# Block 0's expert rows start behind three heads' query columns, the rest standing between its rows

## The reference, cut to what matters

```python
def peer_ffn(h, w_q, sub_k1, sub_k2, u_tab, v_tab):
    q = (h @ w_q).reshape(B, S, PEER_HEADS, 2, PEER_HALF)
    s1 = jnp.einsum('bshd,hnd->bshn', q[..., 0, :], sub_k1)
    s2 = jnp.einsum('bshd,hnd->bshn', q[..., 1, :], sub_k2)
    v1, i1 = lax.top_k(s1, PEER_TOPK)
    v2, i2 = lax.top_k(s2, PEER_TOPK)
    ...
    top_s, pos = lax.top_k(cand_s, PEER_TOPK)
    idx = jnp.take_along_axis(cand_i, pos, axis=-1)
    wts = jax.nn.softmax(top_s, axis=-1)
    ...
        act = jax.nn.gelu(jnp.einsum('thkd,td->thk', u_tab[ib], xb), approximate=False)
        return jnp.einsum('thk,thkd->td', act * wb, v_tab[ib])

for i in range(DEPTH):
    mix = token_mixer(h, ...)
    h = layer_norm(DEEPNORM_ALPHA * h + mix, ln1_g[i], ln1_b[i])
    ffn = peer_ffn(h, peer_wq[i], peer_k1[i], peer_k2[i], peer_u[i], peer_v[i])
    ple = jax.nn.sigmoid(h @ ple_gate[i]) * (p[i] @ ple_proj[i])
    h = layer_norm(DEEPNORM_ALPHA * h + ffn + ple, ln2_g[i], ln2_b[i])
```

## Time and profile before

| | us |
|---|---|
| median of 3 runs | 2176.77 |
| lowest, highest | 2174.72, 2176.99 |
| profiled execution, span | 2174.5 |
| busy: PE, DVE, ACT, POOL | 1833.6, 1416.6, 1025.8, 760.4 |
| gathered rows, share of 16 DMA engines over the span | 59.3% |
| weights and the like, same | 15.5% |

### The profile page before, as it was taken

One profiled execution on the slowest core, in us unless ns is written; L12 is line 12 of the kernel. 1 busy time (PEld: TensorE's weight loads), 2 busy tenths in 40 slices (PEclk: granted clock), 3 DMA queues, 4 the chain that ended last, 5 costly groups with the idle time before them and its releaser, 6 DMA issues. The chain is left out here.

```text
span 2174.5 us, 29162 instructions
## 1 busy us (share of the span) xinstructions
PE 1833.6 (84%) x7040; PEld 1080.4 (50%) x7040; DVE 1416.6 (65%) x3386; ACT 1025.8 (47%) x2321; POOL 760.4 (35%) x604
## 2 busy tenths in 40 slices
PE   8999998978778788788799999989787887888776
PEld 7987776932222222223288877769322322322222
DVE  5764465587777777776567535555877776877764
ACT  5743444444454444445347344544545544444443
POOL 0010000135555556665300100001466565565562
PEclk9999999999999999999989999999999999999999
DMA  7411444689999999999744124446799999999996
GB/s 258 143 60 60 153 137 146 221 351 427 428 427 428 427 426 428 428 427 428 330 139 146 46 78 136 140 161 242 289 427 428 428 427 427 427 428 427 428 427 292
DMA packets 105487, 656.28 MB, mean 302 GB/s; under 512 B 11712, under 2 KB 11840, under 8 KB 39232
## 3 DMA queue, kind: packets, MB, share of 16 engines
q0 software_dynamic: 74592, 542.36, 59.3%
q1 hardware_dynamic: 30816, 112.91, 15.5%
HBM read 654.17 MB, written 1.05 MB: 301 GB/s over the span
## 5 line engine op out<-in xcount | busy, mean ns | idle before, releaser
L567 PE MATMUL acc<-arena 128*128 128x512 f32 x1536 | 755.8, 622 | 239.3 <-ACT arena L898 238.4
L487 POOL DMA_INDIRECT arena<-experts_dram,stage x384 | 541.3, 1410 | 337.0 <-PE acc L567 228.1
L1215 DVE CUSTOM_DVE_ANT_0 arena<-arena,h 128x1024 f32<-128x1024 f32 x384 | 471.1, 1227 | 253.2 <-DMA arena<-experts_dram,stage 163.0
L567 PEld LDWEIGHTS acc<-arena 128*128 128x128 f32 x1536 | 270.2, 192 | 713.8 <-issue 712.9
L892 ACT ACTIVATE gel<-dots 128x1 f32<-128x1 f32 x512 | 103.1, 201 | 519.6 <-DVE dots L1215 519.0
L1121 DVE TENSOR_TENSOR raw_r<-raw,w_hi 128x1024 fp32r<-128x1024 f32 x200 | 236.6, 1221 | 148.0 <-ACT w_hi L834 146.8
L567 PE MATMUL acc<-hidden,arena 128*128 128x512 f32 x512 | 251.9, 627 | 27.2 <-ACT arena L898 25.8
L834 ACT ACTIVATE w_hi<-raw 128x1024 fp32r<-128x1024 f32 x200 | 202.8, 1053 | 126.6 <-DMA raw<-weights_dram 96.7
L898 ACT ACTIVATE arena<-cst,gw 128x128 f32<-128x128 f32 x512 | 205.6, 402 | 88.1 <-ACT gw L895 41.9
L487 POOL DMA_INDIRECT hidden<-experts_dram,stage x128 | 161.4, 1261 | 136.4 <-PE acc L567 101.4
L1215 DVE CUSTOM_DVE_ANT_0 hidden<-hidden,h 128x1024 f32<-128x1024 f32 x128 | 156.9, 1228 | 66.5 <-issue 39.5
(11 more groups left out here) (248 smaller groups left out, 2241.7 us busy)
## 6 DMA issues: line engine op xcount, KB each, us to landing
raw<-weights_dram SPq DMA_DIRECT2D x208, 512.0 KB, 3.4
arena<-experts_dram,stage POOLq DMA_INDIRECT x384, 13.7
lnr<-lnrows_dram POOLq DMA_DIRECT2D x4, 1024.0 KB, 5.2
hidden<-experts_dram,stage POOLq DMA_INDIRECT x128, 13.7
cst<-consts_dram SPq DMA_DIRECT2D x1, 1640.0 KB, 15.1
par<-params_dram POOLq DMA_DIRECT2D x2, 616.0 KB, 10.5
h<-x_dram SPq DMA_DIRECT2D x2, 512.0 KB, 5.2
out_dram<-h SPq DMA_DIRECT2D x2, 512.0 KB, 5.3
```

Of the source, the lines that this page charges most:

```text
L487: nc.gpsimd.indirect_dma_start(slots[i % RING][:, :], None, experts[:, :], bass.IndirectOffsetOnAxis(stage[:, i:i + 1], 0)).then_inc(slot_ ...
L567: last = mm(acc[:, c * 512:(c + 1) * 512], diag[:, i % 4, :], slots[i % RING][:, D + c * 512:D + (c + 1) * 512], start=False, stop=ends)
L1215: nc.vector.tensor_tensor_reduce(slots[s][:, 0:D], slots[s][:, 0:D], h[:, b, :], 1.0, 0.0, ALU.mult, ALU.add, dots[:, i:i + 1]).then_inc(d ...
```

## The change

Only two `wq` halves and then one more stand ahead of the rows of block 0: heads 0, 1 and 2 (`("wq", 0, 0)`, `("wq", 0, 1)`, `("wq", 1, 0)`), with their scores and the selections of heads 0 and 1. The rows of block 0 become steps of the list, `("row", r, i)`, written out and not looped. Between them stand the other five query halves (behind row 3 of heads 0 to 4), their scores (behind row 6) and the four gate steps (behind rows 3 and 9 of heads 5 and 6, one block at a time). Since `hidden` is still read, block 0 uses six slots (`EARLY_RING`); block 1 uses eight in the order `LATE_SLOTS`. `qpT` moves to the place of `emb_gate` and holds four heads. The key pieces become four of half the size, and the weight splits follow their steps two at a time. Query, scores and gate compute the same.

```diff
@@ -71,6 +71,8 @@
 NPARAM = Q_PT + 2 * T
 
 RING = 8
+EARLY_RING = 6
+LATE_SLOTS = (6, 7, 2, 3, 4, 5, 0, 1)
 RANKS = EH * TOPK
 AHEAD = 2
 SELECT_LINKS = 20
...
@@ -123,15 +125,19 @@
     s += [("mT", b, q) for b in range(2) for q in range(2)]
     s += [("out", 0, 0), ("out", 0, 1), ("out", 1, 0), ("ln1", 0), ("out", 1, 1), ("ln1", 1)]
     s += [("pp", 0, 0), ("pp", 1, 0), ("h1T", 0, 0), ("h1T", 0, 1), ("pp", 0, 1), ("h1T", 1, 0), ("h1T", 1, 1), ("pp", 1, 1)]
-    s += [("wq", u, p) for u in range(2) for p in range(2)] + [("sc", b, g) for g in range(2) for b in range(2)]
-    s += [("select", 0), ("texp", 0), ("wq", 2, 0), ("wq", 2, 1), ("wq", 3, 0), ("wq", 3, 1)]
-    s += [("sc", b, g) for g in range(2, 4) for b in range(2)]
-    s += [("pg", 0, 0), ("pg", 0, 1), ("select", 1), ("texp", 1), ("pg", 1, 0), ("pg", 1, 1)]
-    s += [("experts", 0), ("ln2", 0), ("experts", 1), ("ln2", 1)]
+    s += [("wq", 0, 0), ("sc", 0, 0), ("sc", 1, 0), ("select", 0), ("wq", 0, 1), ("sc", 0, 1), ("sc", 1, 1), ("texp", 0)]
+    s += [("select", 1), ("wq", 1, 0), ("sc", 0, 2), ("sc", 1, 2), ("texp", 1)]
+    beside = {(hd - 3, 3): [("wq", hd // 2, hd % 2)] for hd in range(3, EH)}
+    beside |= {(hd - 3, 6): [("sc", 0, hd), ("sc", 1, hd)] for hd in range(3, EH)}
+    beside |= {(5 + c, 3 + 6 * b): [("pg", c, b)] for c in range(2) for b in range(2)}
+    for r in range(EH):
+        for i in range(TOPK):
+            s += [("row", r, i)] + beside.get((r, i), [])
+    s += [("ln2", 0), ("experts", 1), ("ln2", 1)]
     return s
 
 
-NO_BANK = {"softplus", "onorm", "ln1", "ln2", "select", "texp", "experts"}
+NO_BANK = {"softplus", "onorm", "ln1", "ln2", "select", "texp", "row", "experts"}
 STEPS = steps()
 FILLS = [s for s in STEPS if s[0] not in NO_BANK]
 NBANK = 6
...
@@ -176,8 +181,16 @@
 def splits():
 
     order = [i for i, g in enumerate(GROUPS) if g[1]]
-    at = {GROUPS[a][0][0]: b for a, b in zip(order, order[1:])}
-    at["out", 1, 1] = at.pop(("out", 1, 0))
+    at = {}
+    for a, b in zip(order, order[1:]):
+        st = GROUPS[a][0]
+        early, late = st[0], st[1]
+        if st[0] == ("out", 1, 0):
+            early = late = ("out", 1, 1)
+        elif st[0][0] not in ("wq", "pg"):
+            late = early
+        at.setdefault(early, []).extend([(b, 0), (b, 1)])
+        at.setdefault(late, []).extend([(b, 2), (b, 3)])
     return at
...
@@ -267,7 +280,7 @@
 
         slots = [at(2 * D * i, 2 * D) for i in range(4)] + [at(21516 + 2 * D * i, 2 * D) for i in range(2)]
         slots += [hidden[:, 2 * D * i:2 * D * (i + 1)] for i in range(2)]
-        qpT = at(4096, 4096).rearrange("p (k t) -> p k t", k=16)
+        qpT = at(18272, 2048).rearrange("p (k t) -> p k t", k=8)
         base = at(8192, 2048).rearrange("p (b d) -> p b d", b=2)
         scs_flat = at(10240, 4096)
         scs = scs_flat.rearrange("p (b l n) -> p b l n", b=2, l=16)
...
@@ -374,6 +387,20 @@
             b, use = place(L, step)
             return bank_drained[b], use + 1
 
+        def early_uses(s):
+
+            return len(range(s, RANKS, EARLY_RING)) if s < EARLY_RING else 0
+
+        def landed(L, n):
+
+            s = n % EARLY_RING
+            return slot_in[s], 16 * (L * (early_uses(s) + 2 * EH) + n // EARLY_RING + 1)
+
+        def late_slot(L, i):
+
+            s = LATE_SLOTS[i % RING]
+            return s, L * (early_uses(s) + 2 * EH) + early_uses(s) + i // RING + 1
+
         def loaded(L, piece):
             n = L * len(PIECES) + PIECES.index(piece)
             return piece_in[n % RAWS], 16 * (n // RAWS + 1)
...
@@ -437,7 +461,8 @@
                     sp.wait_ge(*used(*stream[n - RAWS]))
                 if n == 4:
                     sp.dma_start(cst[:, C_ID + P:], consts[:, C_ID + P:]).then_inc(consts_in, 16)
-                sp.dma_start(raw[:, n % RAWS, :], weights[L * len(PIECES) + PIECES.index(piece)]).then_inc(piece_in[n % RAWS], 16)
+                cols = 512 if GROUPS[piece[0]][0][0][0] == "sc" else PIECE
+                sp.dma_start(raw[:, n % RAWS, 0:cols], weights[L * len(PIECES) + PIECES.index(piece)][:, 0:cols]).then_inc(piece_in[n % RAWS], 16)
             for b in range(NB):
                 sp.wait_ge(h2_ready, (DEPTH - 1) * NB + b + 1)
                 sp.dma_start(out[b * P:(b + 1) * P, :], h[:, b, :]).then_inc(out_sent, 16)
...
@@ -466,10 +491,22 @@
                     if step == ("select", 0):
                         pool.wait_ge(h1_ready, NB * (L + 1))
                         pool.dma_start(lnr[:, :], lnrows[L, 1]).then_inc(ln_in, 16)
+                    if kind == "row":
+                        _, r, i = step
+                        n = r * TOPK + i
+                        if i == 0:
+                            pool.wait_ge(idx_ready, L * NB * EH + r + 1)
+                        pool.wait_ge(row_used, L * NB * RANKS + n + 1 + RING - EARLY_RING)
+                        nc.gpsimd.indirect_dma_start(
+                            slots[n % EARLY_RING][:, :], None, experts[:, :],
+                            bass.IndirectOffsetOnAxis(idxu[:, n:n + 1], 0)).then_inc(slot_in[n % EARLY_RING], 16)
+                        if n == RANKS - 1 and L + 1 < DEPTH:
+                            pool.wait_ge(*filled(L, ("pp", 1, 1)))
+                            pool.dma_start(par[:, :], params[L + 1]).then_inc(params_in, 16)
                     if kind == "experts":
                         b = step[1]
...
@@ -549,13 +582,28 @@
             ends = [None, None]
 
             for L in range(DEPTH):
-                for step in FILLS + [("experts", 0), ("experts", 1)]:
+                for step in STEPS:
                     kind = step[0]
+                    if kind == "row":
+                        _, r, i = step
+                        n = r * TOPK + i
+                        if n == 0:
+                            if L:
+                                pe.wait_ge(acc_drained, L * NB)
+                            for c in range(2):
+                                mm(acc[:, c * 512:(c + 1) * 512], zero, cst[:, 0:512], start=True, stop=False)
+                        pe.wait_ge(diag_ready, L * NB * RANKS + n + 2)
+                        for c in range(2):
+                            last = mm(acc[:, c * 512:(c + 1) * 512], diag[:, i % 4, :], slots[n % EARLY_RING][:, D + c * 512:D + (c + 1) * 512], start=False, stop=n == RANKS - 1)
+                        last.then_inc(acc_filled if n == RANKS - 1 else row_used, 1)
+                        if n == RANKS - 1:
+                            pe.wait_ge(acc_filled, L * NB + 1)
+                            pe.sem_inc(row_used, 1)
+                        continue
                     if kind == "experts":
                         b = step[1]
                         n0 = (L * NB + b) * RANKS
-                        if L or b:
-                            pe.wait_ge(acc_drained, L * NB + b)
+                        pe.wait_ge(acc_drained, L * NB + b)
                         for c in range(2):
                             mm(acc[:, c * 512:(c + 1) * 512], zero, cst[:, 0:512], start=True, stop=False)
...
@@ -874,6 +925,22 @@
                         act.wait_ge(top_ready, L * 2 * EH + step[1] + 1)
                         AC(texp, texp, ACT.Exp).then_inc(texp_ready, 1)
                         continue
+                    if kind == "row":
+                        _, r, i = step
+                        n = r * TOPK + i
+                        n0, g0 = L * NB * RANKS, L * NB * EH
+                        if i == 0:
+                            act.wait_ge(idx_ready, g0 + r + 1)
+                        act.wait_ge(dot_ready, n0 + n + 1)
+                        AC(gel[:, i:i + 1], dots[:, i:i + 1], ACT.Gelu).then_inc(dot_used, 1)
+                        act.wait_ge(dot_used, n0 + n + 1 + TOPK)
+                        link(AC(gw[:, i:i + 1], gel[:, i:i + 1], ACT.Copy, scale=wts[:, n:n + 1]))
+                        act.wait_ge(row_used, n0 + n + RING - 3)
+                        AC(diag[:, i % 4, :], ident, ACT.Copy, scale=gw[:, i:i + 1]).then_inc(diag_ready, 1)
+                        if i == 12:
+                            act.wait_ge(top_ready, g0 + r + AHEAD + 1)
+                            AC(texp, texp, ACT.Exp).then_inc(texp_ready, 1)
+                        continue
                     if kind == "experts":
                         n0 = (L * NB + step[1]) * RANKS
                         g0 = (L * NB + step[1]) * EH
...
@@ -1186,19 +1252,35 @@
                             layer_norm(base[:, b, :], b, L * 4 + 2 + b + 1, h2_ready)
                         continue
                     if kind == "select":
-                        if step[1] == 0:
-                            dve.wait_ge(*drained(L, ("sc", 0, 0)))
+                        dve.wait_ge(*drained(L, ("sc", 0, step[1])))
                         n = links[0]
                         for _ in select_head(L, step[1]):
                             pass
```

(20 more changed lines are left out.)

82 lines of the change are left out of this document (36 added, 46 removed).

## The result

| | before | after |
|---|---|---|
| median, us | 2175.83 | 2217.63 |
| lowest, highest (4 runs each) | 2174.72, 2176.99 | 2214.07, 2221.63 |
| profiled execution, span | 2174.5 | 2212.7 |
| first dot of block 0, layers 0 and 1 | 451.97, 1533.60 | 400.71, 1500.88 |
| last dot of block 0, layer 0 | 761.51 | 780.32 |

The ratio is 1.019, with a 95% interval of 1.0174 to 1.0206: slower by 1.9%, 41.8 us. The prediction said slower, by 20: the sign and the range (2165 to 2226) hold, the size is twice the forecast one. The page of the changed kernel: span, DMA's busy tenths and rate in 40 slices (the rate of before is the earlier trace rows), then groups of the rows and landings of DMA.

A forecast was written before the change was run, and what follows sets the result against it. Expert rows were taken as bound by their DMA transfers. Per layer, block 0 ends 368.6 + 1.5 - 309.5 - 50.5 = +10.1 us later; twice that makes span 2194.7, plus 2.3 gives 2197 us, range 2165 to 2226.

The forecast's parts named there:

- The start: Chain ahead of block 0's rows: first dot at 401.5 us instead of 452.0, a move of -50.5 us per layer.
- The check named for layer 1: Sign in the profile: layer 1's first dot of block 0 would stand near 1483 us.
- the two gaps of 8 to 10 us on VectorE: Sign in heads 5 and 6: VectorE idle ahead of the gate's multiply, with DMA well under 1 there.
- The query holds: Heads 0 to 4, behind row 3: 2.2 us lost per head at query half and scores, 44.2 us a head.
- ACT's order: In query holds ACT drains the query half before touching row 4, whose matmuls start at 12.1 us, not 5.0.
- The gate holds: Heads 5 and 6, behind rows 3 and 9: VectorE waits for ACT's sigmoid; heads take 58 and 54.2 us.
- the late piece: Head 5: last weight piece needs a raw slot the second hold frees; row 10's dot some 4 us later.
- The slack of six slots: Block 0's ring: a refill may come 3.1 us late before DMA runs dry; with eight slots 8.
- Starved restarts: Rival, chance 0.2: PE's clock falls and first gathers run slow after each hold, +15 us per layer, 2227 us.
- cheap query holds: Rival, chance 0.13: weights fill gaps of heads 0 to 4 (42.0 us each), late piece in time, 2167 us.
- Short landing: Rival, chance 0.1: a gather lands in 4.4 us instead of 6.3, slack 5 us, -9 per layer, 2179 us.
- All hidden: Rival, chance 0.07: every hold fits the ring and only DMA work counts, -26 per layer, 2124 us.

The follow-up runs named there:

- the last kernel of the hold experiments: Changed kernel with gate steps and weight splits moved later, query halves drained behind row 6, each query half and gate block cut in two: 2142.3 us, ratio 0.9851.

## Why the prediction was right or wrong

**The start: right.** First dot at 400.71 us against 401.5. Selection began at 375.23 (375.8), gathers went out at 386.03 (386.3). The check named for layer 1, 1483, had a slip in it, since it left out that layer 1 itself starts later; 1500.88 less the 18.2 of layer 0 is 1482.7. Of the other signs, the two gaps of 8 to 10 us on VectorE show in head 6 (8.84 and 10.07 us); in head 5 splits stand in them.

**The query holds: mechanism right, size short by 5.7 us per layer.** The first term to fail is head 0, taken as 44.2 like the rest and measured at 47.6. The sum put the cost of the start into the first three rows, which ran from slots already filled and took 5.6 us. The cost came behind them: the first reissue was 2.4 us late, and from 406 to 411 DMA moved 61 GB/s (above). No hold is needed for it: in the kernel before with six in flight head 0 takes 41.7 us from row 3 to row 3, where its others take 39.2 to 40.9 (PE's clock is 0.50 over its first rows too, so the shorter ring and the restart are not told apart). The other four were 44.3 to 45.1. From 446 to 625 us a head moved 403 GB/s x 44.8 us = 18.0 MB, 42.2 us at 428, so 2.6 us were lost per head, 2.2 by the forecast. The lost time doesn't lie in a gap of 1.5 and one of 0.7 us but in 15 us at a reduced rate. The runs with five and four in flight show such a rate without any hold.

**ACT's order: right.** Draining three rows later took 1.7 of these 2.6 us away per head in layer 0.

**The gate holds: mechanism right, short by 3.2 and 2.6 us.** By the dots of head 6: first hold 11.8 us against 12.1, rows 4 to 9 8.9 against 10.4, second hold 13.2 against 12.1, and from row 10 to the next row 3 22.9 against 19.6. So two terms were too small and one too large, which hid a part of it. The second hold was taken to be like the first, but the rows ahead of it went through PE at a granted clock near 0.5 to 0.6 at first, so that PE reached the gate block later; the forecast paid for PE's restart once, at the start, and at no hold. The last stretch was priced at VectorE's own pace, "whatever DMA can do", and there VectorE waited for gathers (2.13 and 2.04 us in the lines above). Head 5 has the same two (21.4 us in the last stretch, 14.5 in the second hold once the late piece is out of the way), and the late piece at 4.6 us against 4. That piece landed 7.7 us behind its issue (660.66 to 668.35), where 5.5 was taken; the 13.9 of the earlier trace rows had other weight pieces ahead of it and not gathers alone.

**The slack of six slots: the step that was wrong, and the one that carried luck.** The 3.1 us treat the landing time as 6.3 whenever DMA isn't full. With five in flight the same sum leaves 0.65 us of slack, and measured it lost 7.8 us per head. That the forecast held to its range is in part luck: the changed kernel happens to have six slots, which without a hold still give 422 GB/s. The same sum, used for the changed kernel with five in flight, gave 2245 to 2253 and missed by more than 23 us.

**The rivals.** "Starved restarts" came closer than the forecast itself: it added 15 us per layer to the 10.1 and gave 2227; measured are 8.7 per layer on top of the 10.1, and 2217.6. Its two parts, PE at a lower clock behind a hold and a reduced rate of the first gathers, both show, in the gate heads the one and in all heads the other. It priced the rate from a single stretch of 2 us. The cheap query holds (2167) are out, since no query head took less than 44.3 us, and that case had 42.0. "Short landing" is out. The rule of the Trainium skill ("DMA: Bandwidth & Descriptors", section "Anatomy of one DMA — SWDGE (gpsimd) path") would give 4.4 us, an estimate by that page; the trace does not agree: the gather issued behind the hold at 467.7 landed in 5.8 us, and with four in flight the median was 6.6 and the shortest 5.3. "All hidden" is out by the DMA rate, yet the last kernel of the hold experiments comes within 18 us of its 2124.

## What to carry to other kernels

A step placed inside a stream costs what the slowest in-order engine that touches both makes of it: look at who drains the step, and put that drain, and all that waits for it, as late as its reader allows; with the late weight splits that was worth 67 us here. Count a ring's depth by the rate that it sustains with work taken away, not by the sum of its idle times, and don't count on a gentle slope: eight and six in flight were nearly alike, five lost a sixth of the rate, four a quarter. When DMA reads as busy, look at its bytes per second too.

## What the runs showed of the hardware

- The rate of these gathers (1.05 MB, 8 KB to a partition) by the number in flight: 428 GB/s with eight, 422 with six, 356 with five, 319 with four, at busy shares of 1.01, 1.01, 0.94 and 0.87. The step between six and five hadn't been expected.
- DMA engines can read as busy at 0.83 to 1.02 and move 295 to 383 GB/s, behind a hold; from 472.5 to 482.5 us with gathers alone.
- With five in flight, over 96 gathers, one landed in 6.5 us in the mean with one other not yet landed, in 8.2 with two and in 8.9 with three.
- PE idle for 4.28 us between rows was granted 0.58 of its clock in the 3 us after, and idle for 12.17 us at the start of the rows 0.50 in the 5 us from 401. In the stretches with five and four in flight its mean was 0.93 and 0.88, with no idle time between rows over 3.5 us (2.0 with eight in flight, mean 0.98).
